# A hybrid attention and recurrence layer: input projections as seven block products ahead of the attentions

## The reference

```python
shift, scale, gate = adaln(c, mod_mix_w, mod_mix_b)      # silu(c) @ w + b, in three
h = rmsnorm(x, norm_mix_g) * (1 + scale) + shift          # x: T x 1024
q, k, v, rx, rg, ga, gb = split(h @ w_in)                 # 512 x 5, 1024 x 2 columns
attn = band_attend(q, k, v)                               # 8 heads of 64, 640 keys per query tile
xc = causal_dwconv(rx, conv_w, conv_b)                    # width 4
r, i = sigmoid(xc @ wa + ba), sigmoid(xc @ wx + bx)       # 8 blocks of 64
a = exp(-8 * r * softplus(-lam))
hseq = scan(a, sqrt(1 - a*a) * (i * xc))                  # over the tokens
rnn = hseq * gelu(rg)
merged = sigmoid(ga) * (attn @ w_branch[:512]) + sigmoid(gb) * (rnn @ w_branch[512:])
x = x + gate * (merged @ w_out)
shift, scale, gate = adaln(c, mod_ffn_w, mod_ffn_b)
h = rmsnorm(x, norm_ffn_g) * (1 + scale) + shift
val, gt = split(causal_dwconv(h @ ffn_up_w, ...))         # width 3, 2 x 2816 columns
x = x + gate * ((val * gelu(gt)) @ ffn_down_w)
y = rmsnorm(x, final_norm_g)
```

## Time and profile before

| | us |
|---|---|
| median of 3 runs | 2993.27 |
| lowest and highest | 2992.86, 2993.77 |
| the profiled execution | 2993.03 |
| its span | 2991.2 |
| start, until the first stage boundary | 123.4 |
| end of the fourth attention | 936.5 |
| end of the merge | 1454.05 |
| up-projection begins and ends | 1690.3, 2491.9 |

### The profile page before, as it was taken

One profiled execution on the slowest core, in us unless ns is written; L12 is line 12 of the kernel. 1 busy time (PEld: TensorE's weight loads), 2 busy tenths in 40 slices (PEclk: granted clock), 3 DMA queues, 4 the chain that ended last, 5 costly groups with the idle time before them and its releaser, 6 DMA issues.

```text
span 2991.2 us, 52747 instructions
## 1 busy us (share of the span) xinstructions
PE 2845.7 (95%) x20144; PEld 1818.3 (61%) x20144; DVE 1543.9 (52%) x2759; ACT 1074.5 (36%) x1973; POOL 49.3 (2%) x37
## 2 busy tenths in 40 slices
PE   5799998998999999999999899999999999999997
PEld 3267467476475444444699566666666666666665
DVE  3756355364554433333478676666666666211112
ACT  4345335344443211111355554444444444100000
POOL 0000000000000000000023100000000000000000
PEclk9899999999999999999999999999999999999999
DMA  7100110011022212212455111111111116433311
GB/s 281 38 34 12 45 45 15 30 45 38 22 117 93 78 58 98 78 64 86 128 133 134 45 57 57 57 57 57 57 57 57 57 62 220 144 93 92 92 40 39
DMA packets 167688, 225.45 MB, mean 75 GB/s; under 512 B 48833, under 2 KB 126145, under 8 KB 165009
## 3 DMA queue, kind: packets, MB, share of 16 engines
q1 hardware_dynamic: 156928, 207.94, 21.2%
q10 hardware_dynamic: 9568, 13.09, 1.3%
q0 software_dynamic: 1072, 2.65, 0.2%
HBM read 162.77 MB, written 63.50 MB: 76 GB/s over the span
## 4 chain that ended last, share of the span: by engine, by line
PE 84%; DVE 7%; ACT 4%; issue 4%; DMA 1%; DVEq 0%; ACTq 0%; SPq 0%
PE ps L2126 44%; PE ps L2098 17%; PE ps L1939 11%; PE ps L1976 3%; PE ps L2016 3%; PE ps L2003 2%; DVE arena L1656 1%; ACT arena L977 1%; PE ps L1990 1%; PE ps L1956 1%; PE ps L1901 1%; ACT arena L848 1%; DVE arena L1317 1%; PE ps L1891 1%; DVE arena L1646 1%
## 5 line engine op out<-in xcount | busy, mean ns | idle before, releaser
L2126 PE MATMUL ps<-arena 128*128 128x352 f16 (+1 forms) x11016 | 1486.6, 297 | 22.3 <-ACTq L1025 6.5
L2126 PEld LDWEIGHTS ps<-arena 128*128 128x128 f16 x11016 | 1025.0, 97 | 482.9 <-DVE arena L1625 6.7
L2098 PE MATMUL ps<-arena 128*128 128x512 f16 (+1 forms) x2880 | 517.6, 342 | 1.7 <-ACTq L889 1.6
L2098 PEld LDWEIGHTS ps<-arena 128*128 128x128 f16 x2880 | 241.3, 97 | 278.1 <-issue 3.9
L1939 PE MATMUL ps<-arena 128*128 128x512 f16 (+1 forms) x1920 | 354.8, 347 | 31.1 <-DVE arena L1317 19.2
L1939 PEld LDWEIGHTS ps<-arena 128*128 128x128 f16 x1920 | 163.5, 99 | 222.5 <-issue 37.1
L1836 DVE SCALAR_TENSOR_TENSOR arena<-ps,arena 128x352 f32<-128x352 f32 (+1 forms) x64 | 30.0, 491 | 352.2 <-PE ps L2126 302.9
L1037 ACT ACTIVATE arena<-ps 128x352 f32<-128x352 f32 x264 | 119.5, 463 | 197.9 <-PE ps L2126 197.9
L841 ACT ACTIVATE arena<-arena 128x640 f32<-128x640 f32 (+5 forms) x136 | 103.7, 763 | 211.7 <-DVE arena L1466 211.7
L1549 DVE SCALAR_TENSOR_TENSOR arena<-ps,arena 128x512 f32<-128x512 f32 (+1 forms) x80 | 47.3, 599 | 254.9 <-PE ps L2098 252.4
L1213 ACT ACTIVATE arena<-arena 128x352 f32<-128x352 f32 x48 | 23.9, 498 | 408.7 <-DVE arena L1836 408.7
(11 more groups left out here) (189 smaller groups left out, 2420.4 us busy)
## 6 DMA issues: line engine op xcount, KB each, us to landing
arena<-in_w_up SPq DMA_DIRECT2D x44, 512.0 KB, 3.9
ffn_hidden<-arena SPq DMA_DIRECT2D x44, 512.0 KB, 3.1
arena<-ffn_hidden SPq DMA_DIRECT2D x5, 3872.0 KB, 19.7
arena<-in_w_in SPq DMA_DIRECT2D x36, 512.0 KB, 4.8
arena<-in_w_mod_rest SPq DMA_DIRECT2D x32, 512.0 KB, 3.2
arena<-in_w_down SPq DMA_DIRECT2D x7, 1408.0 KB, 6.3
arena<-mixer_outputs SPq DMA_DIRECT2D x8, 1056.0 KB, 9.0
arena<-in_x_cols SPq DMA_DIRECT2D x12, 704.0 KB, 4.6
```

Source lines behind the costliest of these rows:

```text
L2098: mm = pe.matmul(out, wt[:, wp, k, :], act_t[:, place[k], hp, t:t + w], start=(k == k0 and m == 0), stop=(k == k1 - 1 and m == 2))
L2126: mm = pe.matmul(out, wt[:, k, wp, :], act_t[:, k, hp], start=(first and k == 0 and n == 0), stop=(last and k == K - 1 and n == 2), skip_g ...
```

## The change

The input x comes in columns (`x_cols`), and the start takes the form of the w_out stage: six column parts p with squares, tree, root, scaling, modulation, high parts, low parts (`square0`, `tree0`, `normed0`, `modulate0`, `high0`, `low0`, `block_sums0` on POOL). The modulation is made on TensorE in column form (`modulation`, 128 fp32 matmuls of two columns). Between the parts TensorE forms the values of all heads, 17 tiles of 24 matmuls x 512 columns (`value_tile`, in six lots, `V_TILES`), which go to HBM.

Then 16 rounds r of seven block products form rx and rg of pair j (r = 4j), ga and gb (4j+1), q and k (4j+2), ga and gb again (4j+3). The recurrence of a pair is cut into six chunks of 353 columns, whose gate matmuls stand in `GATE_SLOTS`. The gate rows become tanh rows (`gate_rows_g`, `gate_rows_v`); gates, queries, keys and recurrent outputs are stored to HBM.

The four attentions follow one another, with two sets of buffers: `heads_in(j)` loads queries, keys, values and bias of a pair. The loop order on ACT is changed: copies of transposed probabilities before exponentials. Of the 32 modulation tiles 16 stand in the attentions (`ada_tile`, four each, in the opening tiles), 16 in the merge (`ADA_MERGE`). The merge has only the products with w_branch, 120 matmuls per output tile, and loads the tanh rows (`merge_tile`); all eight low parts of w_out are made there (`OUT_SPLITS`). From the w_out stage on nothing else is different.

```diff
+        V_TILES = ((0, 8), (1, 9), (2, 3, 10, 11), (4, 12), (5, 13), (6, 7, 14, 15, 16))
+        V_ORDER = [i for lot in V_TILES for i in lot]
...
+        ADA_MERGE = (3, 3, 3, 3, 2, 2, 0, 0)
+        def ada_before(f):
+            return NJ * ADA_ATT + sum(ADA_MERGE[0:f])
+        OUT_SPLITS = ((), (), (), (0,), (1,), (2,), (3, 4, 5), (6, 7))
...
+            def round_tiles(r):
+                if r:
+                    sp.wait_ge(p_lo, 7 * r)
+                for i in range(2):
+                    sp.dma_start(praw[i], a["w_proj"][2 * r + i].rearrange("p k m -> p (k m)")).then_inc(p_loaded[i], 16)
...
+            def gate_row(r, g):
+                sp.wait_ge(th_ready[g], r // 2 + 1)
+                row, f = (rowUv, rowUg)[g], r // 2
+                sp.dma_start(th_d[f, :, g, 0:TP], row[:, 3:3 + TP]).then_inc(th_stored[g], 16)
+                sp.dma_start(th_d[f, :, g, TP:T], row[:, TP + 6:LU]).then_inc(th_stored[g], 16)
...
+            def heads_in(j):
+                b = j % 2
+                s = at_loaded[b]
+                for g, half in enumerate((slice(0, 64), slice(64, 128))):
+                    for h in range(2):
+                        sp.dma_start(qs[b][half, h, :], q_d[j, 64 * h:64 * h + 64, (h + g) % 2]).then_inc(s, 16)
+                    for to, part in ((khh[b], 0), (kll[b], 1)):
+                        for t0, t1, k0 in ((0, TP, 0), (TP, T, TP + PAST)):
+                            sp.dma_start(to[half, :, k0:k0 + t1 - t0],
+                                         k_d[j, :, part, t0:t1].rearrange("(h p) t -> p h t", p=64)).then_inc(s, 16)
+                sp.dma_start(vv[b][:, 0:NT, :], v_d[0:NT, :, P * j:P * j + P].rearrange("i p d -> p i d")).then_inc(s, 16)
+                sp.dma_start(vv[b][0:TS, NT + 4, :], v_d[NT, 0:TS, P * j:P * j + P]).then_inc(s, 16)
+                sp.dma_start(vv[b][:, NT:NT + 4, :], a["cache_v"][:, :, j, :].rearrange("c p d -> p c d")).then_inc(s, 16)
+                sp.dma_start(bias[b], band_d[:, 2 * j:2 * j + 2, :]).then_inc(bias_loaded, 16)
...
+            def merge_tile(f):
+                if f >= 2:
+                    sp.wait_ge(d_split, f - 1)
+                    sp.wait_ge(d_dve, 10 * (f - 1))
+                sp.dma_start(dst[f % 2], a["w_branch"][f]).then_inc(d_loaded[f % 2], 16)
+                sp.dma_start(th[f % 2], th_d[f]).then_inc(th_loaded[f % 2], 16)
...
+                    copy(r, 3, q)
+                if i == 0:
+                    root(j, 0)
+                if i == 1:
+                    rnn_hi(j, 2)
+                    gates(j, 3)
+                    tap(j, 4)
+                if i == 2:
+                    rnn_hi(j, 5)
+                if r + 1 < NR:
+                    proj_hi(r + 1, 4)
+                if i == 0:
+                    gates(j, 1)
+                if i == 1:
+                    root(j, 3)
+                    rnn_hi(j, 3)
+                if kind_of(r) == GATES:
+                    gate_rows_v(r)
+                if i == 2:
+                    q_hi(j)
+            for q in range(3):
+                c21(NR - 1, q)
+            gate_rows_g(NR - 1)
...
+            def ada_tile(n):
+                dve.wait_ge(dmw_loaded, 16 * n + 16)
+                for s in range(2):
+                    ins = dve.tensor_tensor_reduce(djunk, dmw, crowv[:, s, :], 0.5, 0.0, ALU.mult, ALU.add,
+                                                   modraw[:, 2 * n + s:2 * n + s + 1])
+                    if s == 0:
+                        chain(ins)
+                ins.then_inc(dm_used, 1)
+                dve.wait_ge(dm_used, n + 1)
...
-                    if p == 3:
-                        split_lo(5 * j + 6, 0)
-                    if p == 4:
-                        split_lo(5 * j + 7, 1)
...
+                        if j == 0:
+                            if p == 2 and h == 1:
+                                dve.wait_ge(crow_sig, 1)
+                                chain(dve.scalar_tensor_tensor(crow, crow_th, 1.0, crow, ALU.add, ALU.mult))
+                            if p > 2:
+                                ada_tile(2 * (p - 3) + h)
+                        elif h == 1 and p:
+                            ada_tile(ADA_ATT * j + p - 1)
...
+            def merge(f):
+                for n, (t, w) in enumerate(BLOCKS):
+                    g, b = 5 * f + n, (5 * f + n) % 2
+                    if n == 0:
+                        dve.wait_ge(th_loaded[f % 2], 16 * (f // 2) + 16)
+                    for m in range(2):
+                        dve.wait_ge(d_filled, 2 * g + m + 1)
+                        if g >= 2:
+                            dve.wait_ge(d_step, g - 1)
+                        dve.scalar_tensor_tensor(sig[:, b, m, 0:w], th[f % 2][:, m, t:t + w], 1.0,
+                                                 ps[:, 4 * b + m, 0:w], ALU.add, ALU.mult).then_inc(d_dve, 1)
+                    dve.wait_ge(d_dve, 2 * g + 2)
+                    if g >= 2:
+                        dve.wait_ge(d_mhi, g - 1)
+                        dve.wait_ge(d_mlo, g - 1)
+                    dve.tensor_tensor(mrg[:, b, 0:w], sig[:, b, 0, 0:w], sig[:, b, 1, 0:w], ALU.add)\
+                        .then_inc(d_step, 1)
+                    if n == 1 and f + 1 < KT:
+                        merge_lo(f + 1)
+                    dve.wait_ge(d_mhi, g + 1)
+                    dve.scalar_tensor_tensor(mstage[:, 1, t:t + w], mrg[:, b, 0:w], 0.5 / WS, mstage[:, 0, t:t + w],
+                                             ALU.mult, ALU.subtract).then_inc(d_mlo, 1)
+                    if n < ADA_MERGE[f]:
+                        ada_tile(ada_before(f) + n)
+                    if f == 5 and n == 3:
+                        gate_columns()
+                    if n >= 2:
+                        for k in OUT_SPLITS[f][n - 2:n - 1]:
+                            out_lo_part(k)
...
+                for f in range(f0, f1):
+                    for k in range(KT):
+                        mm = pe.matmul(ps[:, 0, 2 * f:2 * f + 2], mw[:, f, k, :], csv[:, k, :],
+                                       start=(k == 0), stop=(k == KT - 1))
...
+                if c == 0:
+                    keep_above_zero(pe, p_c21, 3 * (r - 1) + q + 1)
...
+            GATE_SLOTS = {(0, 3): 0, (0, 5): 1, (1, 2): 2, (1, 4): 3, (1, 6): 4, (2, 2): 5}
+            for r in range(NR):
+                for c in range(7):
+                    for q in range(3):
+                        proj_product(r, c, q)
+                    if (r % 4, c) in GATE_SLOTS:
+                        gate_products(r // 4, GATE_SLOTS[r % 4, c])
...
-            def adaln_tile(it, i):
-                n = 8 * it + i
-                if i == 0:
-                    dve.wait_ge(dm_kept, it + 1)
-                dve.wait_ge(dmw_loaded, 16 * n + 16)
-                for s in range(2):
-                    dve.wait_ge(dm_step, 2 * n + s + 1)
-                    ins = dve.tensor_tensor_reduce(djunk, dmw, crow[:, s, :], 1.0, 0.0, ALU.mult, ALU.add,
-                                                   dsum[:, 2 * i + s:2 * i + s + 1])
-                    ins.then_inc(dm_step, 1)
```

2010 lines of the change are left out of this document (1100 added, 910 removed).

## The result

The changed kernel takes 3135.73 us in the median (3131.22 to 3139.11), the kernel before 2993.25: a ratio of 1.0472 with a 95% interval from 1.0459 to 1.0484. It is slower by 142.5 us. The prediction said slower, at 3040, and its range ended at 3088. The profiled execution took 3139.11 us, 3.4 more than the median, and all views of the changed kernel are of it.

A forecast was written before the change was run, and what follows sets the result against it. TensorE was taken to bound projections and merge. Start 253, rounds 602.7, recurrent gates 29.4 and stalls 17, less 933.4, give -31.3; attentions +53.2, merge +32.6 and w_out -7 make +47.5: 3040 us, range 2955 to 3088.

The forecast's parts named there:

- the rounds: Sixteen rounds of 252 block matmuls at 149.5 ns take 602.7 us in place of 685.4: -82.8.
- the w_out stage: Final stage: waits of 5.19 and 1.24 us for low parts at its start go, -7 us.
- DVE's load in the merge: Merge: DVE's instructions and waits for ACT set 26.3 us per output tile with three modulation tiles, 207 us in all.
- the work of the modulation tiles: Opening tiles of the attentions: DVE's modulation work adds 9 us per attention, 36 in all.
- the contention in the start: Start: four DVE low steps beside POOL's sums take 9 us per column part; one takes 0.88 alone, 2.07 shared.
- The stall between rounds: Before each round 4j+2, TensorE waits 4.3 us for copies behind the gate row's tanh on ACT: 17 in all.
- the other twelve rounds: Rival: table loads cost twice or a block waits for gate-row stores, 4 us in each: 3088 us, chance 0.10.
- ACT's order: Attentions: copying transposed probabilities before the next exponentials takes a middle query tile from 5.04 to 4.84 us.
- Merge, +32.6: Merge without gate projections: DVE sets the pace, 207 us against 174.4 for TensorE; ends 175 and 225.
- Attentions, +53: Passage and four attentions: 399.5 us against 346.3, from DVE's modulation work and late modulation loads.
- the start: Until the first round: 253 us, 66 for coefficients and 187 for column parts and values; ends 205 and 270.
- The rivals: Modulation tiles free, 2935, chance 0.22; queues do less harm, no change, 2992, 0.07; other rounds late, 3088, 0.10.

The follow-up runs named there:

- the run with the old order: Exponentials before copies of transposed probabilities in the middle query tiles, against the kernel issuing an attention's modulation tiles before the next pair's loads: 3092.90 us.
- the tiles first: Changed kernel with SyncE issuing an attention's four modulation tiles ahead of the next pair's 15 loads: 3084.14 us.
- the run with the tiles first and short sums: Kernel issuing modulation tiles before the next pair's loads, with only 8 of 1024 columns summed in the attentions' 16 tiles: 3046.04 us.
- the first of the four kernels: Changed kernel with merge stores by halves, six modulation tiles per attention in spread halves, next pair's loads in five lots, eight merge tiles: 2983.00 us.

## Why the prediction was right or wrong

**Right.** The sign, and the stages whose price came from rows of the same instruction: the rounds (16 x 252 x 149.5 ns), the w_out stage, DVE's load in the merge once the store is out of the way (210.1 against 207), the work of the modulation tiles (38 against 36), the contention in the start. The stall between rounds was real: a wait of 2.73 us in each of four, not 4.3, but with the lower clock behind it some 3.5 (from one to the next it is 161.5 us, of which 150.7 are rounds and 7.35 gate matmuls), 14 in all where 17 were forecast. The rule on the cost of a table load that the prediction cites from the Trainium skill ("ScalarE: Activation LUTs", section "What ACT_TABLE_LOAD costs"), and which would have made it longer, doesn't hold here: the row above has 1.28 us for the load, the instruction before it ends at 352.88 and the one behind starts at 354.19, so there is no drain to be seen. None of the other twelve rounds was late.

**Luck: ACT's order.** The prediction took a middle query tile from 5.04 to 4.84 us. In the second attention, from which the 5.04 is, it takes 5.01 in the changed kernel and 5.07 with the old order put back. That the run with the old order was 8.8 us longer, where 9 were costed, doesn't bear the step out.

**Wrong: the step "Merge, +32.6".** It summed DVE's instructions and their waits for ACT within an output tile, and of the DMAs it costed only the gate rows' rate ("no limit"). That the staging buffer has one copy, and its store must land before the next tile's first block, was not in it. In the kernel before the same wait is there (`act.wait_ge(m_stored, 64 * f + 64)`, L925) and no view shows it; all waits of ACT's high part in that merge are put down to DVE:

```profile
ACT arena L927 <- DVE arena L1552: 210.2, 39, 6.1
```

The reason can be worked out: the first block of the next tile has 72 matmuls (a fifth of 64.3 us or more) before ACT may want the buffer, two thirds of them gate projections, and the store lands in 3.3 us. The change left 24 of them, which run ahead of DVE anyway, and put a 2 MB load ahead of the store. 49 of 52 us are shown to be this.

**Wrong in size: "Attentions, +53".** The cause is the one named. The waits for tiles were set down with 17, 12 and 12 us, spacing included, and come to 55.8, of which three are 20.4, 15.6 and 17.0. The term that was too small is the rate: it reckoned 5.2 MB ahead of the tile at about 300 GB/s, some 18 us, and the DMA engines, though busy 0.99 of the time, moved 197 GB/s for the 19.8 us until the tile was issued; it landed after 26.6. Whether the short pieces or the number of loads made that rate wasn't tried. With the tiles first these waits fell from 55.8 to 6.0 us. That is 15 of the 31 us. The other 15 are the attentions without the sums of the modulation: 334.3 us in the run with the tiles first and short sums (6.3 of them still waits for tiles), where the sum has 312 and 7 for the rows of c. A middle query tile was 4.9 to 5.0 us rather than 4.84, 6 us in all, so most of this lies in the opening and last tiles, which was not tried further.

**Wrong in size: the start.** "Coefficients: 53 us at best, 82 at worst; I take 66." They came at about 90: the loads let TensorE begin at 34, not at 22, and the narrow matmuls took the upper price, 54.7 of 27 to 58, though the granted clock reads 1.00 there and not the half on which that price stood. The middle was taken between two ends where nothing spoke for a middle. The other 182 us of the start were forecast at 187.

**The range.** The rivals asked whether known waits would be longer or shorter. None had a wait that the kernel before already contains and hides, and none let two terms miss in the same direction.

## What to carry to other kernels

When a change removes work between a store and the next use of its buffer, price every wait of the kernel before that showed no time: what hid it may be what you remove. Price the bytes ahead of a transfer by the rate that such loads got in a trace, not by the best one (197 here against 377), and put what an engine waits for in its own queue ahead of what is only needed a stage later. Work on an engine with idle time is cheap only where each gap is longer than the piece: 2.6 us in short query tiles cost nearly all of their length, 1.3 us in the long ones about a quarter.

## What the runs showed of the hardware

- Issuing a 32 KB load took 9.75 us on SyncE when it stood behind a load of 1 MB in 512-byte pieces; the issues around it took 0.6. In the first of the four kernels, where it is issued 10 us behind the second half of that load, it took 0.47.
- While those loads ran, the DMA engines were busy 0.99 of the time at 197 GB/s; the 0.5 MB tile and the loads just ahead of it went at 314.
- Behind a wait of 2.73 us of TensorE the granted clock read 0.65 for 3.3 us and 0.86 for the next 4; behind one of 0.79 it read 1.00.
- A store of 512 KB on ACT's queue lands 3.3 us after its issue (median), or 10.6 when 2 MB were issued on SyncE's queue 0.4 us before.
- An fp32 matmul of 128 x 128 weights with two columns moving takes two records of 214 ns; with two columns as weights and 512 moving, two of 480 ns. For a matrix times two vectors the second form did in 31 us what took 55.
- Taking GpSimd's additions away made DVE's low steps 0.84 us each in place of 2.16.
